# Two heads of an attention mixed with split values as weights, in a transformer of two blocks on one core

## The reference

```
z = u @ w_in
qa, ka, va, qb, kb, vb, ga, gb = split(z)        # 512 x3, 512, 128, 128, 1024, 1024
ya = neighbourhood_attention_2d(qa, ka, va, rpb) # 8 heads of 64
yb = windowed_gqa_sink(rope(qb), rope(kb), vb, sink)   # 8 heads, 2 key/value groups
merged = sigmoid(ga) * (ya @ w_branch_a) + sigmoid(gb) * (yb @ w_branch_b)
h = h + merged @ w_out
```

## Time and profile before

| | us |
|---|---|
| median of three runs | 956.73 (956.7 to 957.53) |
| the profiled execution | 956.81 |
| its span, first to last instruction | 955.0 |
| TensorE busy | 947.9 (99%) |
| VectorE busy | 662.6 (69%) |
| ScalarE busy | 533.9 (56%) |
| GpSimd busy | 63.2 (7%) |

### The profile page before, as it was taken

One profiled execution on the slowest core, in us unless ns is written; L12 is line 12 of the kernel. 1 busy time (PEld: TensorE's weight loads), 2 busy tenths in 40 slices (PEclk: granted clock), 3 DMA queues, 4 the chain that ended last, 5 costly groups with the idle time before them and its releaser, 6 DMA issues.

```text
span 955.0 us, 14016 instructions
## 1 busy us (share of the span) xinstructions
PE 947.9 (99%) x5438; PEld 831.6 (87%) x5438; DVE 662.6 (69%) x850; ACT 533.9 (56%) x685; POOL 63.2 (7%) x100
## 2 busy tenths in 40 slices
PE   9999999999999999999999999999999999999997
PEld 8999988888888888898888888999888898888886
DVE  6778869865765566588656666878787586565665
ACT  7577678535544444475445445679674464444544
POOL 2200000001000000022221000100110020000000
PEclk9999999999999999999999999999999999999999
DMA  9684444554765655547666655545435556655541
GB/s 306 205 259 135 133 133 143 209 177 132 251 205 183 196 200 176 178 160 238 211 211 199 212 176 176 174 139 173 133 132 177 176 178 198 209 185 182 190 158 45
DMA packets 117441, 173.17 MB, mean 181 GB/s; under 512 B 3153, under 2 KB 89441, under 8 KB 117393
## 3 DMA queue, kind: packets, MB, share of 16 engines
q1 hardware_dynamic: 115824, 168.32, 54.5%
q0 software_dynamic: 1424, 3.91, 1.3%
q10 hardware_dynamic: 144, 0.26, 0.1%
HBM read 171.44 MB, written 1.05 MB: 181 GB/s over the span
## 4 chain that ended last, share of the span: by engine, by line
PE 99%; DVE 0%; ACT 0%; issue 0%
PE pair L704 22%; PE pair L707 11%; PE acc L686 10%; PE acc L688 10%; PE acc L687 10%; PE pair L686 8%; PE pair L688 8%; PE pair L687 8%; PE acc L1062 1%; PE acc L1211 1%; PE pair L914 1%; PE pair L863 1%; PE acc L1234 1%; PE acc L831 1%; PE acc L897 1%; PE acc L750 0%
## 5 line engine op out<-in xcount | busy, mean ns | idle before, releaser
L704 PE MATMUL pair<-actp,wh 128*128 128x512 f32 x912 | 292.9, 396 | 0.0
L1784 DVE TENSOR_TENSOR wl<-raw,wh 128x2048 fp32r<-128x2048 f32 x89 | 204.8, 2302 | 63.1 <-ACT wh L1328 63.1
L1328 ACT ACTIVATE wh<-raw 128x2048 fp32r<-128x2048 f32 x88 | 168.3, 1912 | 84.2 <-PE acc L688 84.2
L707 PEld LDWEIGHTS pair<-actp,wl 128*128 128x128 f32 x912 | 171.6, 188 | 39.7
L707 PE MATMUL pair<-actp,wl 128*128 128x256 f32 x912 | 179.2, 278 | 0.0
L1779 DVE TENSOR_TENSOR wl<-raw,wh 128x2048 fp32r<-128x2048 f32 x68 | 155.4, 2288 | 31.3 <-ACT wh L1322 30.8
L1322 ACT ACTIVATE wh<-raw 128x2048 fp32r<-128x2048 f32 x69 | 132.0, 1914 | 69.7 <-PE pair L688 45.5
L704 PEld LDWEIGHTS pair<-actp,wh 128*128 128x128 f32 x912 | 141.7, 189 | 1.4
L1541 ACT ACTIVATE arena<-pair 128x512 f32<-128x512 f32 x57 | 34.0, 597 | 170.8 <-PE pair L704 170.8
L686 PE MATMUL acc<-wh,midh 128*128 128x512 f32 x310 | 121.0, 390 | 0.0
L688 PE MATMUL acc<-wh,midl 128*128 128x512 f32 x310 | 120.8, 390 | 0.0
(11 more groups left out here) (352 smaller groups left out, 1386.9 us busy)
## 6 DMA issues: line engine op xcount, KB each, us to landing
raw<-in_w_in SPq DMA_DIRECT2D x37, 1024.0 KB, 5.2
raw<-in_mlp_w SPq DMA_DIRECT2D x32, 1024.0 KB, 5.2
raw<-in_ffn_w_gate SPq DMA_DIRECT2D x22, 1024.0 KB, 5.4
raw<-in_ffn_w_up SPq DMA_DIRECT2D x22, 1024.0 KB, 5.3
raw<-in_ffn_w_down SPq DMA_DIRECT2D x22, 1024.0 KB, 5.1
raw<-in_w_out SPq DMA_DIRECT2D x8, 1024.0 KB, 4.9
raw<-in_w_up_rnn SPq DMA_DIRECT2D x4, 1024.0 KB, 5.1
raw<-in_cmp_k_w SPq DMA_DIRECT2D x2, 1024.0 KB, 5.8
```

What stands on the lines that cost most here:

```text
L704: return nc.tensor.matmul(bank[:, :].rearrange("p (u t) -> p u t", u=2), h[:, k, cs], actp[:, :, k, :], **kw)
L707: return nc.tensor.matmul(bank[:, 0:T], l[:, k, cs], acth[:, k, :], **kw)
L1328: nc.scalar.activation(wh[:, n % R, :], raw[:, n % R, :], ACT.Copy).then_inc(hi_ready, 1)
L1784: nc.vector.tensor_tensor(wl[:, n % R, :], raw[:, n % R, :], wh[:, n % R, :].bitcast(F32), ALU.subtract).then_inc(lo_ready, 1)
```

## The change

`FV = 6` is the first head that is mixed in the second way. For heads 6 and 7 the probabilities are scaled by VectorE ahead of the turn, copied as `pth`, their low half made as `ptl`, and the mix takes its weights from `vns`, a new split copy of the two heads' values (ScalarE and VectorE, at panel 5). The outcomes go to `y3`, already transposed, so the second turn of outcomes has only two transposes; ScalarE and VectorE split the bank's half and `y3` apart. ScalarE's "grouped" order begins one panel earlier, at panel 10. The diff:

```diff
@@ -196,6 +196,8 @@
         prob3 = carve(13800, TT, T + 1)
         pth, ptl = mrgl[:, 4:6, :], mrgl[:, 6:8, :]
         ylow = thr
+        y3 = carve(12544, T)
+        vns = midl[:, 4:6, :].rearrange("p k t -> p (k t)").rearrange("p (k h s d) -> p k h s d", k=TT, h=2, s=2)
         vbs = midh[:, 4:6, :].rearrange("p k t -> p (k t)").rearrange("p (k g s d) -> p k g s d", k=TT, g=GR, s=2)
         atok2 = carve(14336, TT, NH * DH)
         ybT = xs[:, 0, :].rearrange("p (k t) -> p k t", t=T)
@@ -370,6 +372,8 @@
         rope_read = sem("rope_read")
         qb_ready = sem("qb_ready")
         vbh_ready = sem("vbh_ready")
+        vnh_ready = sem("vnh_ready")
+        vn_ready = sem("vn_ready")
         vb_ready = sem("vb_ready")
         scaled = sem("scaled")
         sink_set = sem("sink_set")
@@ -642,7 +646,8 @@
             if k < NH:
                 kh, kl = keys2(h // 4)
                 return (qst[:, h, :], kh[:, h % 4, :], kl[:, h % 4, :],
-                        [va[:, kt, DH * h:DH * (h + 1)] for kt in range(TT)])
+                        [va[:, kt, DH * h:DH * (h + 1)] for kt in range(TT)] if h < FV else
+                        [vns[:, kt, h - FV, :, :].rearrange("p s d -> p (s d)") for kt in range(TT)])
             g = h // 4
             return (qst[:, h, :], mrgl[:, g, :], mrgl[:, GR + g, :],
                     [vbs[:, kt, g, :, :].rearrange("p s d -> p (s d)") for kt in range(TT)])
@@ -656,6 +661,7 @@
             return ps[TURNED[0]][:, 0:T] if j == 3 else ps[3][:, 0:T]
 
         OUT_A = 5
+        FV = 6
         LOW, HIGH, LAST = (0, 1), (4, 5), (6, 7)
         GATE_BANKS = (HIGH, LOW)
         UPA_BANKS = (LAST, HIGH)
@@ -1198,25 +1204,27 @@
                 m.then_inc(scored, 1)
 
             def turn2_(k):
-                if k < NH:
+                if k < FV:
                     pe.wait_ge(exped, NH + k + 1)
                 else:
-                    pe.wait_ge(scaled, k - NH + 1)
-                if k <= NH:
+                    pe.wait_ge(scaled, k - FV + 1)
+                if k <= FV:
                     pe.wait_ge(probT_ready, NH + k)
                 else:
-                    pe.wait_ge(ptl_ready, k - NH)
+                    pe.wait_ge(ptl_ready, k - FV)
                 for i in range(4):
-                    tt, kt = (i // 2, i % 2) if k < NH else (i % 2, i // 2)
+                    tt, kt = (i // 2, i % 2) if k < FV else (i % 2, i // 2)
                     m = nc.tensor.transpose(ps[3][:, i * P:(i + 1) * P], prob_of(k)[:, tt, kt * P:(kt + 1) * P], ident)
                 m.then_inc(turned, 1)
 
             def mix2(k):
                 vt = head2(k)[3]
                 pe.wait_ge(normed, NH + k)
-                if k >= NH:
-
-                    pe.wait_ge(ptl_ready, k - NH + 1)
+                if k >= FV:
+
+                    pe.wait_ge(ptl_ready, k - FV + 1)
+                    if k == FV:
+                        pe.wait_ge(vn_ready, 1)
                     if k == NH:
                         pe.wait_ge(vb_ready, 1)
                     for kt in range(TT):
@@ -1285,9 +1293,11 @@
                     pe.wait_ge(vb_ready, 1)
                     turn_out(OUT_A, atok2, 0)
                 if n == GA2 + 3:
-                    pe.wait_ge(normed, 2 * NH)
+                    pe.wait_ge(normed, NH + FV)
                     pe.wait_ge(midl_ready, 2)
-                    turn_out(OUT_A, atok2, 2)
+                    for tt in range(TT):
+                        m = nc.tensor.transpose(ps[OUT_A][:, tt * P:(tt + 1) * P], atok2[:, tt, 2 * P:3 * P], ident)
+                    m.then_inc(atok_turned, 1)
 
             for u in range(2):
                 for br, (ah, al) in enumerate(((midh, midl), (acth, actl))):
@@ -1609,7 +1619,7 @@
                 act.wait_ge(turned, NH + k + 1)
 
                 act.wait_ge(mixed, NH + k)
-                to = probT2[:, :] if k < NH else pth.rearrange("p k t -> p (k t)")
+                to = probT2[:, :] if k < FV else pth.rearrange("p k t -> p (k t)")
                 nc.scalar.activation(to, ps[3][:, :], ACT.Copy).then_inc(probT_ready, 1)
 
             def low_rows(k):
@@ -1639,7 +1649,7 @@
                 m.then_inc(exped, 1)
 
             def heads2_turned(n, part):
-                if mix_at.get((n, part), 0) >= NH:
+                if mix_at.get((n, part), 0) >= FV:
                     low_rows(mix_at[n, part])
                 if (n, part) in turn_at:
                     copy2(turn_at[n, part])
@@ -1670,7 +1680,7 @@
                                                  scale=hrstd[:, tt:tt + 1]).then_inc(ev, 1)
 
             for n in range(QKV2, F2):
-                grouped = GA2 + 2 <= n <= BR
+                grouped = GA2 + 1 <= n <= BR
                 if grouped:
                     heads2_turned(n - 1, 1)
                 if n == BR:
@@ -1713,6 +1723,10 @@
                     for tt in range(TT):
                         nc.scalar.activation(va[:, tt, :], ps[GATE2_BANKS[0][tt]][:, :], ACT.Copy,
                                              scale=rstd[:, tt:tt + 1]).then_inc(va_evac, 1)
+                if n == VA2 + 3:
+                    act.wait_ge(va_evac, 2)
+                    nc.scalar.activation(vns[:, :, :, 0, :], va[:, :, DH * FV:DH * NH].rearrange("p k (h d) -> p k h d", h=2),
+                                         ACT.Copy).then_inc(vnh_ready, 1)
                 if n - 1 in (QB, QB + 1):
                     u = n - 1 - QB
                     act.wait_ge(qb_evac, u + 1)
@@ -1733,8 +1747,13 @@
                     gates2(n)
                 heads2_scored(n, 0)
                 if n in (GA2 + 1, GA2 + 4):
-                    i = (n - GA2 - 1) // 3
-                    out_hi(midh, i, OUT_A, 1 + i + 1)
+                    if n == GA2 + 1:
+                        out_hi(midh, 0, OUT_A, 2)
+                    else:
+                        act.wait_ge(atok_turned, 3)
+                        nc.scalar.activation(midh[:, 2, :], ps[OUT_A][:, 0:T], ACT.Copy)
+                        act.wait_ge(normed, 2 * NH)
+                        nc.scalar.activation(midh[:, 3, :], y3, ACT.Copy).then_inc(midh_ready, 1)
                 if not grouped:
                     gates2(n)
 
@@ -2264,10 +2283,11 @@
                                         pth.rearrange("p k t -> p (k t)").bitcast(F32), ALU.subtract).then_inc(ptl_ready, 1)
 
             def norm2(k):
-                if k >= NH:
-
-                    dve.wait_ge(ylow_ready, k - NH + 1)
-                    nc.vector.tensor_tensor(ybT[own(k % 2), (k - NH) // 2, :], ps[4][0:DH, 0:T], ylow[0:DH, :],
+                if k >= FV:
+
+                    dve.wait_ge(ylow_ready, k - FV + 1)
+                    to = y3 if k < NH else ybT[:, (k - NH) // 2, :]
+                    nc.vector.tensor_tensor(to[own(k % 2)], ps[4][0:DH, 0:T], ylow[0:DH, :],
                                             ALU.add).then_inc(normed, 1)
                     return
                 dve.wait_ge(mixed, NH + k + 1)
@@ -2282,11 +2302,11 @@
             def heads2(n, part):
                 if (n, part) in score_at:
                     mask2(score_at[n, part])
-                if turn_at.get((n, part), 0) >= NH:
+                if turn_at.get((n, part), 0) >= FV:
                     low_probs(turn_at[n, part])
                 if (n, part) in mix_at:
                     norm2(mix_at[n, part])
-                if scale_at.get((n, part), 0) >= NH:
+                if scale_at.get((n, part), 0) >= FV:
                     scale2(scale_at[n, part])
 
             def rope(x, swapped, r1, r2, width, done_count):
@@ -2375,13 +2395,21 @@
                                                         mrgl[own(g), g, :].bitcast(F32), ALU.subtract)
                     m.then_inc(kst_ready, 1)
                 heads2(n, 0)
+                if n == VA2 + 3:
+                    dve.wait_ge(vnh_ready, 1)
+                    nc.vector.tensor_tensor(vns[:, :, :, 1, :], va[:, :, DH * FV:DH * NH].rearrange("p k (h d) -> p k h d", h=2),
+                                            vns[:, :, :, 0, :].bitcast(F32), ALU.subtract).then_inc(vn_ready, 1)
                 if n == QB + 1:
                     dve.wait_ge(vbh_ready, 1)
                     nc.vector.tensor_tensor(vbs[:, :, :, 1, :], ps[OUT_A][:, 0:T].rearrange("p (k g d) -> p k g d", k=TT, g=GR),
                                             vbs[:, :, :, 0, :].bitcast(F32), ALU.subtract).then_inc(vb_ready, 1)
                 if n in (GA2 + 1, GA2 + 4):
-                    i = (n - GA2 - 1) // 3
-                    out_lo(midl, midh, i, OUT_A, 1 + i + 1)
+                    if n == GA2 + 1:
+                        out_lo(midl, midh, 0, OUT_A, 2)
+                    else:
+                        dve.wait_ge(midh_ready, 3)
+                        nc.vector.tensor_tensor(midl[:, 2, :], ps[OUT_A][:, 0:T], midh[:, 2, :].bitcast(F32), ALU.subtract)
```

(1 more changed line is left out.)

## The result

| | before | changed |
|---|---|---|
| median of 8 runs each, us | 956.72 (956.31 to 957.53) | 959.80 (958.84 to 960.48) |
| profiled execution, us | 956.81 | 959.29 |
| its span, us | 955.0 | 956.8 |

The ratio is 1.0032, with an interval of 1.0024 to 1.0041: slower by 3.1 us. I had forecast 958.4 with a range of 956.9 to 959.7 and "no change" as the likeliest (up to 958.6). The direction was right, the forecast loss of 1.7 us was about half of what came, the range missed the median by 0.1, and by the prediction's own bound the kernel is slower and not unchanged.

The account below looks back on a forecast made before the run. TensorE, 99% of the last chain at full clock, was taken as the bound. Terms -0.72 - 0.17 + 2.09 + 0.38 = +1.58 us on 956.81 gave 958.4 us, range 956.9 to 959.7.

Parts of the forecast that it names:

- The gain on TensorE: Mixes of heads 6 and 7 save 0.72 us, two dropped transposes in the second turn of outcomes about 0.17: -0.89.
- The rule of four passes: Skill's rule that true FP32 takes four array passes; by it alone the mixes save nothing; the prediction followed the trace instead.
- The stall at turn 6: Head 6's transposes on TensorE wait for VectorE's scaling behind the rotation, starting at 666.90 for 664.81: +2.09 us.
- The stall at turn 7: Head 7's transposes on TensorE wait for VectorE's scaling until 674.60: a further +0.38 us, bounds 0 and 0.9.
- What stays covered: Mixes 6 and 7, turn 8, panel 12 and the casts of the two heads' values: costed at nothing on TensorE.
- Turn 8: Head 8's transposes on TensorE: two paths, 7.42 and 7.5 us from turn 7, even within error; nothing, bounds 0 to 0.3.
- The first rival: VectorE's backlog goes on past turn 7, delaying turn 7 by 0.7 and turn 8 by 0.3: 959.0 us, chance 0.22.
- follows 0.06 behind its scaling without a row: Turn 14 in the kernel before, without a row among TensorE's waits: cited against VectorE's backlog going on.
- Nothing covers it: Turn 6's wait counts in full, as TensorE is in order and later steps stand behind it: 2.09 us.
- The rival for it: The stall drops TensorE's clock to 1.2 GHz for half a panel, adding some 2.8 us: 961.2 us, chance 0.06.
- It has no idle stretch of 2 us today, and the one of 1.2 us left the clock full: TensorE's idle time in the kernel before, the 1.2 us at the start; stated in the rival of a falling clock.
- 956.81 + 1.58: Profiled execution of the kernel before plus the summed terms gives 958.4 us, time outside the span taken as unchanged.

Follow-up runs that it names:

- e9_work_no_wait: Kernel before plus VectorE's reciprocal and two scalings of head 6 behind the rotation, TensorE not waiting for them: 956.89 us, ratio 1.0002.
- e1_again: The changed kernel run once more without any edit, against the kernel before: 959.87 us, ratio 1.0035.
- e3_no_scaling: Changed kernel with the scaling of heads 6 and 7 left out, output not right: 955.92 us, ratio 0.9991 to the kernel before.
- e4_reorder: Complete changed kernel; scalings ahead of query low halves and rotation, ScalarE's swap behind exponentials, first outcomes split a panel later: 956.07 us, ratio 0.9994 to before.
- e8_reorder2: e4_reorder plus VectorE scaling heads 8 and 14 ahead of writing outcomes of heads 7 and 13: 956.27 us, ratio 0.9995 to the kernel before.

## Why the prediction was wrong, point by point

- The gain on TensorE: right. Forecast -0.89; the trace after has 0.47 for each mix in place of 0.84 and 0.82, and 0.21 less for the transposes, together 0.93, of which the small wait at turn 8 takes 0.16. The rule of four passes, by which the mixes would save nothing, does not hold here.
- The stall at turn 6: right in place and size, 2.10 us against 2.09, and undone by moving the scaling. The stall at turn 7: right, 674.65 against 674.60, in executions at full clock.
- "What stays covered": right for the casts. Turn 8 was costed at nothing and took about 0.2. The first rival, a backlog that goes on, did not come: turn 14 starts 712.95 - 711.19 = 1.76 later than before, and turn 8 1.96 later, the difference being the transposes. But its evidence was misread. That turn 14 "follows 0.06 behind its scaling without a row" was taken as no wait, and it is one of some 0.2 us.
- The step that failed is "Nothing covers it": I priced a wait of TensorE at its length. In 10 of 14 executions of the changed kernel the clock falls behind it, and the spans of these are 0.6 to 1.2 us longer, one 2 (I count by the gap in the spans, since a mean clock of 0.998 alone is found before too; six of the ten have 0.996 or 0.997, and one of them is shown in a trace; the other four go by the span alone). The rival for it had the mechanism right, at a chance of 0.06 where the runs have 10 of 14, and at a price of 2.8 us where the trace has 1.6, of which 0.4 is given back at turn 7, 1.2 net. "It has no idle stretch of 2 us today, and the one of 1.2 us left the clock full" was the very row that said the case was open, and I read it as evidence against.
- The second failed step is "956.81 + 1.58": the time outside the span was carried over from before. It is 1.74 to 1.94 there and 1.90 to 3.05 in the changed kernel (medians 2.44 and 2.05 in two sets of runs), so 0.2 to 0.6 us of the loss. That an edit without any stall can raise it by 0.3 is shown by e9_work_no_wait. All kernels made from the changed one have it at 1.8 to 2.6 or more from one execution to the next, with a wide spread, and those made from the kernel before have a narrow one, at 1.8 or at 2.2. Why is open.

Together, by the means of 14 executions against 22, the loss is 3.07 us: 2.54 in the span, of which 1.86 is gain and stalls at full clock (the four executions without a fall) and 0.68 the clock, and 0.53 outside it. The traces agree where the start of each is taken out. From the start of mix 5 to the end of the span:

| trace | us |
|---|---|
| before; e9_work_no_wait | 291.0; 291.0 |
| changed, full clock | 292.8 |
| changed, clock fallen (e1_again) | 293.9 |
| e3_no_scaling; e4_reorder | 290.3; 290.2 |
| e8_reorder2 | 289.8 |

So the change as built costs 1.8 us and a further 1.1 when the clock falls; in the other order it gains 0.8, and 1.2 with the two turns served first.

## What to carry to other kernels

On an engine that is busy 99% of the time a new wait of 2 us is not priced by its length: the matmuls behind it may run at half the clock, in some executions only, so compare the spans and clocks of all executions and not only the profiled one. A table of waits leaves out waits of 0.2 us that records overlap; distances from start to start show them. Where an added small step has to be ready for the bottleneck engine, ask what stands ahead of it in its own engine's list and on the engine that feeds it; here moving the scalings, one low half and one swap gave back the whole stall at the same work. Moving only the scalings split the wait in three.

## What the runs showed of the hardware

- TensorE's granted clock went from 1.0 to 0.5 behind a stall. No execution of 11 shows it at 1.4 us; in some executions of the same program it came at 2.1, and in all five at 4. It fell during the steps that follow, not during the idle time: in e1_again the matmuls of the first microsecond behind the stall (666.60 to 667.57) still have their full pace, and then those of 512 columns start every 0.43 us for 0.23.
- The granted clock is 0.50 in the last 2 us of the span of before, without a matmul, and 0.78 in those of the changed kernel, so a mean of 0.998 does not tell a fall in the middle from one at the end.
- Three more VectorE instructions with their waits took 0.3 us more outside the span with an equal span, 2.11 to 2.27 in 11 executions; two more in another place took none.
- Four transposes directly behind a wait take 0.41 us to the next step, and 0.36 otherwise.
